# The first conditioning unit and the first chunk of the input projection cover one k-tile in place of two

## The chip, the cores and the metric

The kernel runs on one core of a Trainium2 chip. The metric is the time of one execution in microseconds (us) on the device; the profile of one execution shows what each engine did in it. Engines are called as the profile calls them: PE (matmul), PEld (its weight loads), DVE (VectorE), ACT (ScalarE), POOL (GpSimd), SP (which issues most transfers).

## The reference, cut to what matters

One decoder layer for 256 prompt rows and 8 x 4 sample rows, 288 rows in all, with D = 2048, which is 16 k-tiles of 128. Only its head is touched here.

```
mod = silu(c) @ w_ada + b_ada                 # 2048 x 12288, 9 different c
shift1, scale1, gate1, shift2, scale2, gate2 = split(mod, 6)
h = x * (1 + scale1) + shift1
proj = h @ w_in                               # 2048 x 5120: 40 output tiles of 128
... attention, gated mixing, w_out, norm, ConvFFN, norm
```

k-tile k of h needs columns k of shift1 and scale1, and each of those needs all 2048 rows of w_ada. The layer then goes on to attention, spatial gating, the output projection and a ConvFFN with the much larger w_up and w_down.

## The kernel before, in words

Everything is held transposed: a k-tile of h is 128 partitions by 288 rows. The work is spread over engines by hand; each engine has a list of its own, in order, and semaphores tie the lists.

**Weights in slabs.** w_in, w_out, w_up and w_down come in slabs of 512 KB (128 x 1024 floats, eight 128 x 128 blocks) into `raw`, four slots. ACT rounds a slab to `wH` (`hi`, L1034), DVE takes the rest, `wL = raw - wH` (`lo`, L1441, which counts `split_done`). h is split the same way into `hH` and `hL`. A block then takes three products on PE: hL x wH, hH x wL, hH x wH (L455 to L457, in `products`). A slab is so 24 products.

**The input projection** goes over five chunks of k-tiles, `CHUNKS`: 2, 2, 4, 4, 4. A slab is two k-tiles by four output tiles, ten slabs for each two k-tiles, 80 in all. An output tile of a chunk builds up in one of five PSUM banks (`ps`, banks 0 to 4 in rotation). PE's `take` waits until the bank was released. The first chunk is copied out to `proj` by ACT (L1252), later chunks are added to it by DVE (L1626). For each slab i DVE's list has the adds of slab i and then lo of slab i + 3; ACT's has hi of slab i + 3 and then the copies of slab i, but for slabs 4, 5 and 6, whose hi stands in one go behind the copies of slab 2.

**Conditioning.** w_ada comes in slabs of 512 KB too, through eight slots. A unit (`MOD_UNITS`) gives a few tiles of shift and of scale. Unit 0 is 8 slabs and gives k-tiles 0 and 1; unit 1 is 8 slabs and gives 2 and 3; the others are 16 slabs for four tiles of each. PE does a slab in 16 records of a matmul with 32 columns of weights (L484 for half units, L471 for whole ones). When a unit is complete, ACT copies it to `adaS` (L1046), PE turns it (L512), DVE adds the bias into `modT` (`mod_finish`, L1452) and makes h (`modulate`, L1473 to L1477, into `H32`), ACT makes hH, DVE makes hL. All of unit 0 stands ahead of the first product of the projection. PE fills its waits there with products whose result is not used (`keep_busy`, L584). Later slabs come in bursts of four between two slabs of the projection (`BURSTS`, the slab index behind which each burst stands: 3, 6, 8, 11, ...), and `TURN_AT` is the slab behind which a unit is turned.

**Loads.** SP issues in this order at the start: conditioning 0 to 3, w_in 0, conditioning 4 to 7, x of two k-tiles, w_in 1 to 3. Then for each slab i the conditioning slabs that fit in the ring, and w_in i + 5 when slab i + 1 has been split. One bias product with its own small loads (L610, `bias`) stands behind slab 2.

## Time and profile before

| | us |
|---|---|
| median of 3 runs | 1392.53 (1391.79 to 1394.35) |
| the profiled execution | 1392.78 |
| its span, first to last instruction | 1391.1 |
| PE busy | 1370.0 (98%) |
| DVE busy | 836.8 (60%) |
| ACT busy | 570.4 (41%) |

The profile's busy time of PE is modelled at the end of each matmul, so the starts of matmuls are the better measure of pace. A timeline merges instructions of a kind that follow each other; the bracket behind a row is the time that the engine sat idle before it and what ended the wait. DMA engines are shared by all queues. 0.2% of the median is 2.8 us.

### The profile page before, as it was taken

How to read it: one execution, taken by the hardware profiler on the slowest of the kernel's cores; microseconds unless marked ns; L12 is line 12 of the kernel's file. 1: busy time of each engine (PE TensorE's matmuls, PEld its weight loads, DVE VectorE, ACT ScalarE, POOL GpSimd, SP SyncE). 2: the span in 40 equal slices, each digit the busy share in tenths (PEclk: the TensorE clock that was granted, in tenths of full speed). 3: DMA queues.
4: the chain of work that ended last, by engine and by line, in shares of the span. 5: the costliest groups of instructions: out<-in, count | busy, mean ns of one | idle time of the engine just before them, and what ended most of it. 6: DMA issues, size and time to landing. Idle time of an engine off the chain costs nothing.

```text
span 1391.1 us, 29223 instructions
## 1 busy us (share of the span) xinstructions
PE 1370.0 (98%) x11397; PEld 1297.9 (93%) x11397; DVE 836.8 (60%) x1404; ACT 570.4 (41%) x848; POOL 105.9 (8%) x250
## 2 busy tenths in 40 slices
PE   7999999999999999999999999999999999999996
PEld 5999898899889888999999999999999999999996
DVE  2475556568876569555665544665665544766755
ACT  4533223254643236633444333443444333444433
POOL 1000000004221000000110000110110000101000
PEclk9999999999999999999999999999999999999998
DMA  9999988975888988885545455455455555455541
GB/s 371 409 339 392 343 332 321 342 276 184 300 310 324 366 310 327 290 306 177 166 141 181 162 166 167 151 162 169 151 169 171 160 164 166 149 178 163 169 150 68
DMA packets 89907, 324.94 MB, mean 234 GB/s; under 512 B 10653, under 2 KB 10653, under 8 KB 89440
## 3 DMA queue, kind: packets, MB, share of 16 engines
q1 hardware_dynamic: 82512, 297.34, 60.4%
q0 software_dynamic: 6880, 24.10, 5.1%
q10 hardware_dynamic: 432, 2.33, 0.4%
q8 instruction: 60, 0.98, 0.3%
q14 instruction: 23, 0.19, 0.0%
HBM read 318.05 MB, written 5.67 MB: 233 GB/s over the span
## 4 chain that ended last, share of the span: by engine, by line
PE 94%; DVE 3%; ACT 1%; issue 1%; DMA 1%; SPq 0%; DVEq 0%; ACTq 0%
PE ps L455 28%; PE ps L456 28%; PE ps L457 28%; PE ps L471 5%; PE ps L798 1%; DVE xT L1886 1%; DVE wL L1441 1%; PE ps L484 1%; PE ps L712 1%; DMA ada<-w_ada 1%; PE ps L662 0%; PE ps L584 0%; DVE xT L1897 0%; ACT wH L1034 0%; PE ps L545 0%
## 5 line engine op out<-in xcount | busy, mean ns | idle before, releaser
L1441 DVE TENSOR_TENSOR wL<-raw,wH 128x1024 fp32r<-128x1024 f32 x372 | 449.6, 1218 | 362.7 <-ACT wH L1034 360.6
L1034 ACT ACTIVATE wH<-raw 128x1024 fp32r<-128x1024 f32 x372 | 389.5, 1053 | 593.5 <-PE ps L457 558.7
L455 PE MATMUL ps<-hL,wH 128*128 128x288 f32 x2016 | 602.6, 299 | 0.9 <-DVE hL L1610 0.5
L456 PE MATMUL ps<-hH,wL 128*128 128x288 f32 x2016 | 600.3, 298 | 0.0
L457 PE MATMUL ps<-hH,wH 128*128 128x288 f32 x2016 | 599.7, 297 | 0.0
L455 PEld LDWEIGHTS ps<-hL,wH 128*128 128x128 f32 x2016 | 380.7, 189 | 15.0 <-issue 10.9
L456 PEld LDWEIGHTS ps<-hH,wL 128*128 128x128 f32 x2016 | 379.9, 188 | 0.5 <-issue 0.5
L457 PEld LDWEIGHTS ps<-hH,wH 128*128 128x128 f32 x2016 | 379.1, 188 | 0.0
L455 PE MATMUL ps<-ffL,wH 128*128 128x288 f32 x688 | 204.8, 298 | 0.0
L456 PE MATMUL ps<-ffH,wL 128*128 128x288 f32 x688 | 203.3, 295 | 0.0
L457 PE MATMUL ps<-ffH,wH 128*128 128x288 f32 x688 | 202.7, 295 | 0.0
L1626 DVE TENSOR_TENSOR proj<-ps,proj 128x288 f32<-128x288 f32 x160 | 71.2, 456 | 106.2 <-PE ps L457 105.7
L455 PEld LDWEIGHTS ps<-ffL,wH 128*128 128x128 f32 x688 | 129.0, 188 | 1.0 <-DVE xT L2012 1.0
L457 PEld LDWEIGHTS ps<-ffH,wH 128*128 128x128 f32 x688 | 129.7, 189 | 0.0
L456 PEld LDWEIGHTS ps<-ffH,wL 128*128 128x128 f32 x688 | 129.2, 188 | 0.0
L455 PE MATMUL ps<-mix,wH 128*128 128x288 f32 x256 | 78.3, 306 | 0.4 <-DVE xT L1712 0.2
L456 PE MATMUL ps<-mix,wL 128*128 128x288 f32 x256 | 75.6, 295 | 0.0
L457 PE MATMUL ps<-mix,wH 128*128 128x288 f32 x256 | 75.5, 295 | 0.0
L2191 POOL COPY E<-U 128x4 f32 (+1 forms) x44 | 9.9, 225 | 734.6 <-ACT U L1347 734.6
L455 PEld LDWEIGHTS ps<-mix,wH 128*128 128x128 f32 x256 | 48.1, 188 | 6.3 <-issue 5.4
L457 PEld LDWEIGHTS ps<-mix,wH 128*128 128x128 f32 x256 | 48.2, 188 | 0.0
L456 PEld LDWEIGHTS ps<-mix,wL 128*128 128x128 f32 x256 | 48.1, 188 | 0.0
(261 smaller groups left out, 972.4 us busy)
## 6 DMA issues: line engine op xcount, KB each, us to landing
raw<-w_up SPq DMA_DIRECT2D x168, 512.0 KB, 3.5
ada<-w_ada SPq DMA_DIRECT2D x96, 512.0 KB, 6.4
raw<-w_down SPq DMA_DIRECT2D x83, 512.0 KB, 3.5
raw<-w_in SPq DMA_DIRECT2D x80, 512.0 KB, 7.3
adaX<-w_ada SPq DMA_DIRECT2D x40, 512.0 KB, 5.4
adaY<-w_ada SPq DMA_DIRECT2D x40, 512.0 KB, 7.2
raw<-w_out SPq DMA_DIRECT2D x32, 512.0 KB, 5.7
KV<-keys POOLq DMA_DIRECT2D x16, 512.0 KB, 5.6
```

The costliest lines, as they stand in the source:

```text
L455: nc.tensor.matmul(out, wH[:, w:w + P], rhs_lo(kk), start=start, stop=False)
L456: nc.tensor.matmul(out, wL[:, w:w + P], rhs_hi(kk), start=False, stop=False)
L457: mm = nc.tensor.matmul(out, wH[:, w:w + P], rhs_hi(kk), start=False, stop=stop)
L471: mm = nc.tensor.matmul(ps[32 * c:32 * c + 32, bank, 0:256], cT[:, 32 * k:32 * k + 32], src[:, 256 * c:256 * (c + 1)], start=(k == 0), sto ...
L484: mm = nc.tensor.matmul(ps[32 * c:32 * c + 32, bank, 0:P], cT[:, 32 * k:32 * k + 32], src[:, 512 * kk + P * c:512 * kk + P * (c + 1)], sta ...
L712: mm = nc.tensor.matmul(ps[32 * hq:32 * hq + 32, hh, 0:P], PTm[:, o:o + 32], KV[buf][:, kt * 1024 + h * P:kt * 1024 + (h + 1) * P], start= ...
L798: mm = nc.tensor.transpose(b[0:n, t * P:(t + 1) * P], tile(S4, t, r * P, r * P + n), ident)
L1034: nc.scalar.activation(wH[:, o:o + cols], raw[:, o:o + cols], ACT.Copy).then_inc(hi_done, 1)
L1441: vec_tt(wL[:, o:o + cols], raw[:, o:o + cols], wH[:, o:o + cols].bitcast(F32), ALU.subtract).then_inc(split_done, 1)
L1626: release(vec_tt(tile(proj, n), ps[:, k % 5, 0:ROWS], tile(proj, n), ALU.add), ("in", c, k))
L1886: steps.link(vec_tt(x, x, spread(b[:, 0:1], [0, 2], [1, ROWS]), ALU.mult))
L2191: copy(spread(e, [18, halves], [1, 2]), spread(U[:, o + SEQ:o + SEQ + 1], [UW, halves], [1, 2]))
```

## The change

Unit 0 is split into two units of four slabs: unit 0 gives k-tile 0, the new unit 1 gives k-tile 1, as a burst behind slab 1. The units behind them move up by one number, the bursts that stood behind slab 3 stand behind slab 4. The first chunk is k-tile 0 alone for output tiles 0 to 23, in three slabs of eight tiles by one k-tile. A mixed chunk follows in slabs 3 to 9: four slabs (3, 5, 7, 9) of four new tiles by both k-tiles, copied out by ACT, and between them three (4, 6, 8) of eight tiles by k-tile 1, added by DVE. The number of slabs stays 80. In slabs 0 to 2, DVE copies out tiles 0 to 2 and ACT tiles 3 to 7. Slab 0 is split in two halves. Up to slab 9, DVE's list has lo of slab i + 2 (not i + 3) behind its adds of slab i, and ACT's has hi of slab i + 2 behind its copies of slab i; slabs 12 and 13 are split at slab 10. SP loads conditioning 0 to 3, w_in 0, one tile of x, w_in 1, conditioning 4 and 5, w_in 2, conditioning 6 and 7, x, w_in 3, x. x beyond the fourth k-tile is issued at slab 9 in place of 7, the bias product stands behind slab 11, and POOL's later loads wait for k-tiles 2 and 3 of h. The weights are laid out in memory in the new order.

```
-CHUNKS = [(0, 2), (2, 2), (4, 4), (8, 4), (12, 4)]
+CHUNKS = [(0, 1), (0, 2), (2, 2), (4, 4), (8, 4), (12, 4)]
 LAST = len(CHUNKS) - 1
+ALONE = 24
 LAST_ORDER = [8, 9, 6, 7, 4, 5, 0, 1, 2, 3]
-def group_of(c, p):
-    return LAST_ORDER[p] if c == LAST else p
-IN_SLABS = [(c, g, half) for c, (_, nk) in enumerate(CHUNKS) for g in range(IN_GROUPS) for half in range(nk // 2)]
+def in_slabs():
+    out = [(0, 0, 1, p, 8, True, True) for p in range(0, ALONE, 8)]
+    p = 0
+    for n in (4, 8, 4, 8, 4, 8, 4):
+        out.append((1, 0, 2, p, n, True, True) if n == 4 else (1, 1, 1, p, n, True, True))
+        p += n
+    for c, (k, nk) in enumerate(CHUNKS[2:], 2):
+        for g in range(IN_GROUPS):
+            for half in range(nk // 2):
+                out.append((c, k + 2 * half, 2, 4 * g, 4, half == 0, half == nk // 2 - 1))
+    return out
+IN_SLABS = in_slabs()
 IN_N = len(IN_SLABS)
+MIXED = [t for j in range(3) for t in [*range(ALONE + 4 * j, ALONE + 4 * j + 4), *range(8 * j, 8 * j + 8)]] + [*range(ALONE + 12, ALONE + 16)]
+def in_tile(c, p):
+    if c == 1:
+        return MIXED[p]
+    return 4 * LAST_ORDER[p // 4] + p % 4 if c == LAST else p
+def in_bank(c, p):
+    return (p + 1) % 5 if c == 0 else p % 5
+IN_TD = [sum(n - 1 for _, _, _, _, n, _, stop in IN_SLABS[:s] if stop) for s in range(IN_N + 1)]
...
+HALF, QUARTER = 8, 4
 ADA_RING, BURST = 8, 4
-MOD_UNITS = [(0, HALF, 0, 16), (8, HALF, 2, 18), (16, 16, 4, 20), (32, 16, 8, 24), (48, 16, G1, G1 + 4), (64, 16, 12, 28),
-             (80, 16, G1 + 8, G1 + 12), (96, 16, SH2, SH2 + 4), (112, 16, SC2, SC2 + 4), (128, 16, SH2 + 8, SH2 + 12),
+MOD_UNITS = [(0, QUARTER, 0, 16), (4, QUARTER, 1, 17), (8, HALF, 2, 18), (16, 16, 4, 20), (32, 16, 8, 24), (48, 16, G1, G1 + 4),
+             (64, 16, 12, 28), (80, 16, G1 + 8, G1 + 12), (96, 16, SH2, SH2 + 4), (112, 16, SC2, SC2 + 4), (128, 16, SH2 + 8, SH2 + 12),
              (144, 16, SC2 + 8, SC2 + 12)]
-GATE_UNITS = (4, 6)
-U_LAST_IN, U_SC2, U_SH2B, U_SC2B = 7, 8, 9, 10
-Q_UP = 11
-PARTS = {1: (1,), 2: (2, 3), 3: (4, 5), 5: (6, 7)}
-BURSTS = [3, 6, 8, 11, 14, 16] + [19 + 5 * k // 2 for k in range(20)] + [S_OUT + 15] + [S_OUT + 17 + 2 * k for k in range(7)]
+GATE_UNITS = (5, 7)
+U_SC2, U_SH2B, U_SC2B = 9, 10, 11
+Q_UP = 12
+PARTS = {2: (1,), 3: (2, 3), 4: (4, 5), 6: (6, 7)}
+BURSTS = [1, 4, 6, 8, 11, 14, 16] + [19 + 5 * k // 2 for k in range(20)] + [S_OUT + 15] + [S_OUT + 17 + 2 * k for k in range(7)]
...
+            def ada_quarter_slab(slot, turn, j, copies, bank):
+                if j == 0 and copies:
+                    pe.wait_ge(adaS_ready, copies)
+                pe.wait_ge(ada_in[slot], turn * 16 + 16)
+                src = ada_slot(slot)
+                for kk in range(2):
+                    for c in range(4):
+                        k = 4 * j + 2 * kk + c // 2
+                        mm = nc.tensor.matmul(ps[32 * c:32 * c + 32, bank, 0:P], cT[:, 32 * k:32 * k + 32], src[:, 512 * kk + P * c:512 * kk + P * (c + 1)],
+                                              start=(j == 0 and kk == 0), stop=(j == QUARTER - 1 and kk == 1))
+                mm.then_inc(ada_used, 1)
...
-            for a in range(HALF):
+            for a in range(QUARTER):
                 ada_next(a)
-                if a >= 2:
+                if a >= 1:
                     keep_busy(ps[:, 0, :], 1)
             pe.wait_ge(small_in, 16 * 2)
             ada_turn(0, ("turn", 0), blocks=1)
-            keep_busy(ps[:, 0, :], 4)
-            for i, (c, g, half) in enumerate(IN_SLABS):
-                k0, nk = CHUNKS[c]
-                k = k0 + 2 * half
-                arriving = None
+            keep_busy(ps[:, 0, :], 3)
+            def second_half(t, kk):
+                if t == 4:
+                    pe.wait_ge(split_done, 1)
+            def second_turn(t, kk):
+                if t == 2:
+                    ada_turn(1, ("turn", 1), blocks=1)
+            for i, (c, k, nk, p0, n, start, stop) in enumerate(IN_SLABS):
                 if i == 0:
-                    arriving = lambda kk: pe.wait_ge(h_ready if kk else h_first, 1)
-                elif g == 0:
+                    pe.wait_ge(h_first, 1)
+                elif i == ALONE // 8:
+                    pe.wait_ge(h_ready, 1)
+                elif c > 1 and p0 == 0:
                     pe.wait_ge(h_ready, k // 2 + 1)
-                banks = [(4 * g + t) % 5 for t in range(4)]
-                products(i, i, lambda kk: tile(hH, (k + kk) % H_SLOTS), lambda kk: tile(hL, (k + kk) % H_SLOTS), banks, half == 0, half == nk // 2 - 1,
-                         taking=lambda t: take(pe, ("in", c, 4 * g + t), banks[t]), arriving=arriving, by_k=i == 0)
+                banks = [in_bank(c, p0 + t) for t in range(n)]
+                products(i, i, lambda kk: tile(hH, (k + kk) % H_SLOTS), lambda kk: tile(hL, (k + kk) % H_SLOTS), banks, start, stop, ktiles=nk,
+                         taking=lambda t: take(pe, ("in", c, p0 + t), banks[t]), between={0: second_half, 2: second_turn}.get(i))
...
-            for a in range(HALF):
-                if a == HALF // 2:
-                    load(0, io["w_in"], 0, 0)
+            def load_x(k, n):
+                sp.dma_start(xT[:, k * ROWS:(k + n) * ROWS], io["xT"][:, k * ROWS:(k + n) * ROWS]).then_inc(x_in[k], 16)
+            for a in range(QUARTER):
                 load_ada(a, a)
-            sp.dma_start(xT[:, 0:2 * ROWS], io["xT"][:, 0:2 * ROWS]).then_inc(x_in, 16)
-            for s in range(1, RING):
-                load(s, io["w_in"], s, s)
-            issued = HALF
+            load(0, io["w_in"], 0, 0)
+            load_x(0, 1)
+            load(1, io["w_in"], 1, 1)
+            for a in range(QUARTER, QUARTER + 2):
+                load_ada(a, a)
+            load(2, io["w_in"], 2, 2)
+            for a in range(QUARTER + 2, 2 * QUARTER):
+                load_ada(a, a)
+            load_x(1, 1)
+            load(3, io["w_in"], 3, 3)
+            load_x(2, 2)
+            issued = 2 * QUARTER
             for i in range(-1, S_UP[0]):
-                limit = ada_through(i - 2) + (BURST if i < 2 else ADA_RING)
+                limit = ada_through(i - 2) + ADA_RING if i > 1 else issued + 2 * (i >= 0)
...
-            hi(0, 0, 0)
             unit_copy(0)
+            act.wait_ge(raw_in[0], 16)
+            nc.scalar.activation(wH[:, 0:SLAB // 2], raw[:, 0:SLAB // 2], ACT.Copy).then_inc(hi_first, 1)
             act.wait_ge(h32_first, 1)
             nc.scalar.activation(tile(hH, 0), tile(H32, 0), ACT.Copy).then_inc(hH_first, 1)
+            nc.scalar.activation(wH[:, SLAB // 2:SLAB], raw[:, SLAB // 2:SLAB], ACT.Copy).then_inc(hi_done, 1)
+            def in_copy(i, t):
+                c, p0 = IN_SLABS[i][0], IN_SLABS[i][3]
+                in_filled(act, i, t)
+                release(nc.scalar.activation(tile(proj, in_tile(c, p0 + t)), ps[:, in_bank(c, p0 + t), 0:ROWS], ACT.Copy), ("in", c, p0 + t))
+            def in_hi(s):
+                hi(s, s // RING, s % RING)
+            in_hi(1)
+            for t in range(3, 8):
+                in_copy(0, t)
+            in_hi(2)
+            for t in range(3, 8):
+                in_copy(1, t)
+            unit_copy(1)
+            in_hi(3)
+            in_copy(2, 3)
             act.wait_ge(h32_ready, 1)
             nc.scalar.activation(tile(hH, 1), tile(H32, 1), ACT.Copy).then_inc(hH_ready, 1)
-            hi(1, 0, 1)
-            act.dma_start(xT[:, 2 * ROWS:4 * ROWS], io["xT"][:, 2 * ROWS:4 * ROWS]).then_inc(x_in, 16)
-            hi(2, 0, 2)
-            for i in range(IN_N + 1):
-                if i not in (1, 2, IN_N):
-                    hi_ahead(0, 0, i)
+            for t in range(4, 8):
+                in_copy(2, t)
+            in_hi(4)
+            for i in range(3, IN_N + 1):
+                if 10 < i < IN_N:
+                    in_hi(i + AHEAD)
                 if i in TURN_AT:
                     unit_copy(TURN_AT[i])
-                if i < IN_GROUPS:
-                    for t in range(4):
-                        k = 4 * i + t
-                        if t < 3:
-                            act.wait_ge(tile_done, 3 * i + t + 1)
-                        else:
-                            act.wait_ge(used, i + 1)
-                        release(nc.scalar.activation(tile(proj, k), ps[:, k % 5, 0:ROWS], ACT.Copy), ("in", 0, k))
-                if i == 2:
-                    hi_ahead(0, 0, 1)
-                    hi_ahead(0, 0, 2)
-                if i == 7:
+                if i < 10:
+                    if IN_SLABS[i][2] == 2:
+                        for t in range(4):
+                            in_copy(i, t)
+                    in_hi(i + 2)
+                if i == 10:
+                    in_hi(12)
+                    in_hi(13)
...
+            def modulate_one(k, signal):
+                dve.wait_ge(x_in[k], 16)
+                dd = by_seq(tiles(H32, k, 1, SEQ, ROWS), 1)
+                a, b = (16 + k) * MODS, k * MODS
+                steps.link(vec_tt(dd, by_seq(tiles(xT, k, 1, SEQ, ROWS), 1), mods(16 + k, 1)[1], ALU.mult))
+                vec_tt(dd, dd, mods(k, 1)[1], ALU.add)
+                vec_ts(tile(H32, k, 0, SEQ), tile(xT, k, 0, SEQ), modT[:, a:a + 1], modT[:, b:b + 1], ALU.mult, ALU.add).then_inc(signal, 1)
+            def mod_finish_one(k):
+                b = filled(dve, ("turn", k))
+                out = spread(modT[:, k * MODS:k * MODS + 1], [16 * MODS, 2], [1, MODS])
+                steps.link(vec_tt(out, spread(b[:, 0:1], [32, 2], [1, MODS]), spread(vec[:, V_ADA + k:V_ADA + k + 1], [16, 2], [0, MODS]), ALU.add))
+                release(vec_tt(out, out, spread(b[:, 64:65], [32, 2], [1, MODS]), ALU.add), ("turn", k))
+                released(dve, ("turn", k))
...
-            lo(0, 0)
-            mod_finish(("turn", 0), (0, 16), n=2)
-            dve.wait_ge(x_in, 16)
-            modulate(0)
+            mod_finish_one(0)
+            modulate_one(0, h32_first)
+            dve.wait_ge(hi_first, 1)
+            vec_tt(wL[:, 0:SLAB // 2], raw[:, 0:SLAB // 2], wH[:, 0:SLAB // 2].bitcast(F32), ALU.subtract).then_inc(lo_first, 1)
             dve.wait_ge(hH_first, 1)
             vec_tt(tile(hL, 0), tile(H32, 0), tile(hH, 0).bitcast(F32), ALU.subtract).then_inc(h_first, 1)
+            dve.wait_ge(hi_done, 1)
+            vec_tt(wL[:, SLAB // 2:SLAB], raw[:, SLAB // 2:SLAB], wH[:, SLAB // 2:SLAB].bitcast(F32), ALU.subtract).then_inc(split_done, 1)
+            for i in range(2):
+                for t in range(3):
+                    in_copy(i, t)
+                lo(i + 1, i + 1)
+            in_copy(2, 0)
+            in_copy(2, 1)
+            mod_finish_one(1)
+            modulate_one(1, h32_ready)
+            in_copy(2, 2)
+            lo(3, 3)
             dve.wait_ge(hH_ready, 1)
             vec_tt(tile(hL, 1), tile(H32, 1), tile(hH, 1).bitcast(F32), ALU.subtract).then_inc(h_ready, 1)
-            lo(1, 1)
-            lo(2, 2)
-            for i in range(IN_N + 1):
+            lo(4, 4 % RING)
+            for i in range(3, IN_N + 1):
                 if i < IN_N:
-                    c, g, half = IN_SLABS[i]
-                    if c and half == CHUNKS[c][1] // 2 - 1:
-                        for t in range(4):
-                            k = 4 * g + t
-                            if t < 3:
-                                dve.wait_ge(tile_done, 3 * (IN_GROUPS * c + g) + t + 1)
-                            else:
-                                dve.wait_ge(used, i + 1)
-                            n = 4 * group_of(c, g) + t
-                            release(vec_tt(tile(proj, n), ps[:, k % 5, 0:ROWS], tile(proj, n), ALU.add), ("in", c, k))
-                if i < IN_N - 1:
+                    c, _, nk, _, n, _, stop = IN_SLABS[i]
+                    if stop and (c > 1 or nk == 1):
+                        for t in range(n):
+                            in_add(i, t)
+                if i < 10:
+                    lo(i + 2, (i + 2) % RING)
+                if i == 10:
+                    lo(12, 12 % RING)
+                    lo(13, 13 % RING)
+                if 10 < i < IN_N - 1:
                     lo(i + AHEAD, (i + AHEAD) % RING)
...
-            pool.wait_ge(h32_ready, 1)
+            pool.wait_ge(h32_ready, 2)
```

## Rows read from the trace of the kernel before

**Rows 1.** The page, part 1: busy time, share of the span, instructions.
```profile
PE 1370.0 (98%) x11397; PEld 1297.9 (93%) x11397; DVE 836.8 (60%) x1404; ACT 570.4 (41%) x848; POOL 105.9 (8%) x250
```

**Rows 2.** Table of windows: length, busy of each engine, PEclk, DMA share, GB/s.
```profile
25.00:60.00 35.00, 35.00 (x371) 32.21 (x370) 13.88 (x18) 22.26 (x46) 0.59 (x1) 1.00 1.03 409
```

**Rows 3.** Timeline of PE from 0 to 20.7: start us, length us, what.
```profile
6.46 1.93 PE L484 MATMUL ps<-ada,cT 128*32 128x128 f32 x32 [6.46 <-ACT cT L1230]
9.24 1.08 PE L484 MATMUL ps<-ada,cT 128*32 128x128 f32 x16 [0.84 <-DMA ada<-w_ada]
10.25 1.22 PE L584 MATMUL ps<-cT 128*128 128x256 f32 x2
11.40 1.08 PE L484 MATMUL ps<-ada,cT 128*32 128x128 f32 x16
...
13.42 0.64 PE L484 MATMUL ps<-adaX,cT 128*32 128x128 f32 x16
```

**Rows 4.** Tile cT from 12.4 to 13.4: ns shortest/median/longest, first and last start.
```profile
L584 PE MATMUL ps<-cT x2: 487/640/793, 12.4 to 13.0; 128*128 128x256 f32 x2
```

**Rows 5.** Timeline of SP's queue from 0 to 110: when transfers were issued.
```profile
3.63 0.50 SPq L944 DMA_DIRECT2D raw<-w_in  x1
...
6.96 1.64 SPq L944 DMA_DIRECT2D raw<-w_in  x3
```

**Rows 6.** DMA issues at 3.63 and at 6.96: KB, us from issue to landing.
```profile
raw<-w_in SPq DMA_DIRECT2D x1, 512.0 KB, 8.1
...
raw<-w_in SPq DMA_DIRECT2D x1, 512.0 KB, 12.0
```

**Rows 7.** Timeline of all engines from 17 to 21.
```profile
17.03 0.64 PE L484 MATMUL ps<-adaY,cT 128*32 128x128 f32 x16
...
17.74 0.28 ACT L1046 ACTIVATE adaS<-ps 128x128 f32<-128x128 f32 x1 [4.91 <-PE ps L484]
...
18.50 0.26 DVE L1452 TENSOR_TENSOR modT<-ps,vec 128x18 f32<-128x18 f32 x2 [4.33 <-PE ps L512]
...
19.20 0.73 DVE L1477 TENSOR_SCALAR H<-xT,modT 128x256 f32<-128x256 f32 x2
19.64 0.44 ACT L1234 ACTIVATE hH<-H 128x288 fp32r<-128x288 f32 x1 [1.62 <-DVE H L1477]
...
20.11 0.46 DVE L1610 TENSOR_TENSOR hL<-H,hH 128x288 fp32r<-128x288 f32 x1 [0.19 <-ACT hH L1234]
...
20.72 0.38 PE L455 MATMUL ps<-hL,wH 128*128 128x288 f32 x1 [0.53 <-DVE hL L1610]
```

**Rows 8.** Timeline of PE around a burst, and around the turn of unit 1.
```profile
34.41 0.30 PE L457 MATMUL ps<-hH,wH 128*128 128x288 f32 x1
...
36.52 0.41 PE L455 MATMUL ps<-hL,wH 128*128 128x288 f32 x1
36.76 0.29 PE L456 MATMUL ps<-hH,wL 128*128 128x288 f32 x1
...
51.70 0.27 PE L512 MATMUL ps<-cst,adaS 128*128 128x128 f32 x1
```

**Rows 9.** Timelines of PE, ACT and DVE where slab 2 ends.
```profile
30.25 0.29 PE L457 MATMUL ps<-hH,wH 128*128 128x288 f32 x1
...
30.58 0.41 ACT L1252 ACTIVATE proj<-ps 128x288 f32<-128x288 f32 x1 [0.38 <-PE ps L457]
30.89 3.06 ACT L1034 ACTIVATE wH<-raw 128x1024 fp32r<-128x1024 f32 x3
...
31.97 3.50 DVE L1441 TENSOR_TENSOR wL<-raw,wH 128x1024 fp32r<-128x1024 f32 x3 [7.08 <-ACT wH L1034]
```

**Rows 10.** Timeline of DVE from 6 to 110.
```profile
64.09 1.22 DVE L1441 TENSOR_TENSOR wL<-raw,wH 128x1024 fp32r<-128x1024 f32 x1
65.22 1.37 DVE L1626 TENSOR_TENSOR proj<-ps,proj 128x288 f32<-128x288 f32 x3
...
95.24 1.55 DVE L1626 TENSOR_TENSOR proj<-ps,proj 128x288 f32<-128x288 f32 x4
```

More of the change, by code:

```diff
@@ L424, in width, with in_filled @@
             return ROWS if k < 8 else SEQ
+        def in_filled(eng, s, t):
+            if t < IN_SLABS[s][4] - 1:
+                eng.wait_ge(tile_done, IN_TD[s] + t + 1)
+            else:
+                eng.wait_ge(used, s + 1)
         def in_done(eng, p):
@@ L440, in products @@
             def products(s, i, rhs_hi, rhs_lo, banks, first, last, ktiles=2, taking=None, arriving=None, by_k=False, between=None):
-                pe.wait_ge(split_done, s + 1)
+                if isinstance(s, int) and s == 0:
+                    pe.wait_ge(lo_first, 1)
+                else:
+                    pe.wait_ge(split_done, s + 1)
                 n = len(banks)
@@ L491, in ada_next @@
                 first, n, _, _ = MOD_UNITS[q]
-                step = ada_half_slab if n == HALF else ada_slab
-                if a == MOD_UNITS[2][0]:
-                    released(pe, "bias")
+                step = {QUARTER: ada_quarter_slab, HALF: ada_half_slab}.get(n, ada_slab)
                 if a == MOD_UNITS[U_SC2][0]:
@@ L1050, in unit_copy @@
                 a, n, _, _ = MOD_UNITS[q]
-                ada_copy(a + n, ada_bank(q), ("turn", q - 1) if q else None, cols=P if n == HALF else 256)
+                ada_copy(a + n, ada_bank(q), ("turn", q - 1) if q else None, cols=256 if n == 16 else P)
             def h_hi(p):
@@ L1642, in _ @@
                         modulate(PARTS[q][0])
[L1643 removed]
+                if i == 13:
                     b = filled(dve, "bias")
@@ L2225, in rows_t @@
         return f(x.T.reshape(-1, P, ROWS).transpose(1, 0, 2).reshape(P, -1))
-    w_in = a["w_in"][0].reshape(KT, P, IN_GROUPS, 4, P)
-    w_in_s = f(np.stack([w_in[CHUNKS[c][0] + 2 * half:CHUNKS[c][0] + 2 * half + 2, :, group_of(c, g)].transpose(1, 0, 2, 3).reshape(P, -1)
-                         for c, g, half in IN_SLABS]))
+    w_in = a["w_in"][0].reshape(KT, P, 4 * IN_GROUPS, P)
+    w_in_s = f(np.stack([w_in[k:k + nk][:, :, [in_tile(c, p0 + t) for t in range(n)]].transpose(1, 0, 2, 3).reshape(P, -1)
+                         for c, k, nk, p0, n, _, _ in IN_SLABS]))
     w_out = a["w_out"][0]
@@ L2256, in ada_slab_of @@
         _, n, first, second = unit
+        if n == QUARTER:
+            return np.concatenate([w_ada[tile_of(4 * j + 2 * kk + odd), cols(t, 1)] for kk in range(2) for odd in range(2) for t in (first, second)], 1)
         if n == HALF:
```

33 lines of the change are left out of this document (20 added, 13 removed).

## The prediction

> **What bounds the kernel now.** I read the page's first part before anything else: PE is busy for nearly the whole span [rows 1]. In the table of windows the stretch right behind the start shows PE without a gap while the DMA engines are full [rows 2]. So what counts is when the first product starts, how much work PE does after it, and where PE has to wait. The timeline of PE gives the first: PE starts at 6.46, works through eight conditioning slabs, each as it lands, and begins the first product of the projection at 20.72 [rows 3, 7]. From there to the end of the third slab at 30.38 (30.25 and one spacing of 0.13) it needs 9.66 us, 3.22 us a slab and 0.40 us for the three products that one k-tile gives to one output tile [rows 7, 9]. The chain of work follows PE almost all the way to the end, so I take a delay near the start to reach the end whole.
>
> **Part 1, the earlier start.** Unit 0 needs four conditioning slabs in place of eight. The third landed at 9.24, when PE took it up [rows 3]. The first slab of w_in was issued at 3.63 and took 8.1 us: 11.7 [rows 5, 6]. The fourth conditioning slab lies between, at about 10.5. SP issues these five in the same order as now. The second w_in slab landed at 6.96 + 12.0 = 19.0, behind four conditioning slabs and 288 KB of x; that makes 1.3 us for each 512 KB [rows 5, 6]. In the new order this gives landings of about 12.1 for the tile of x, 13.4 (w_in 1), 14.7 and 16.0 (conditioning 4, 5), 17.3 (w_in 2), 18.6 and 19.9 (6, 7), 20.3 (x), 21.6 (w_in 3).
>
> PE reaches conditioning slab 3 later than it lands, because slabs 0 and 1 end at 8.4 and a keep-busy product now follows slab 1 as well. One conditioning slab takes 1.01 us and a keep-busy product 1.15 us early on; after 13.4 a slab takes 0.57 us [rows 3]. The granted clock reads 1.00, that is 2.4 GHz, but those durations are nearly two to one, like 1.2 to 2.4 GHz, and one keep-busy product shows the step inside it: its first half took 793 ns and its second, at 13.0, 487 [rows 4]. Before that step PE had worked without a gap since 9.24. Now it works without one from 6.46. If the step comes as long after the gapless work began (3.8 us), it is at 10.2, slab 3 runs from 11.1 to 11.7; if it stays at 13.0, slab 3 ends at 12.7 (8.4 + 1.15 + 1.01 + 1.15 + 1.01). From the end of the last slab (17.60) to the first product (20.72) the kernel now takes 3.12 us: ACT's copy at 17.74, VectorE's at 18.50, ScalarE's hH at 19.64, hL at 20.11 [rows 7]. The new path has the same links; the half lo beside hH adds some 0.1 us. So the first product starts at 14.9 or at 16.0 (the late keep-busy product adds 0.1). I take the middle, 15.4: **-5.3 us**, ends -5.8 and -4.7.
>
> **Part 2, what moves behind the start.** Unit 1's four slabs now run as a burst behind slab 1. A burst moves the next slab from 34.54 to 36.52, and the product behind it starts 0.24 us later in place of 0.13: **+2.1 us** [rows 8]. They land by 19.9 and are wanted from about 21.9, so they cost no wait. One more transposition of 0.27 us, most of it hidden under the neighbours [rows 8]: **+0.1**. The product for the bias moves from slab 2 to slab 11 and costs the same there. The number of products and of slabs is unchanged.
>
> **Part 3, the first wait, for k-tile 1.** Call B the start of slab 2. VectorE copies tiles 0 and 1 of it (until B + 1.56, with 0.46 for a copy, by its add from PSUM [rows 10]), makes the factors and h of k-tile 1 (1.14 us, from 18.50 to 19.64 [rows 7]), copies tile 2 (to B + 3.0), does lo of slab 3 (next instruction 1.13 us later [rows 10], B + 4.1), hL (0.46), and 0.15 us later PE can start: B + 4.6. Without it slab 3 would start at B + 3.4. **+1.3 us** with the slow first product. Ends: 1.0 if VectorE's copies take only the 0.36 us at which its adds follow each other [rows 10], 1.6 if each of the three handovers between engines takes 0.1 us longer. The trace of before has no copy of such a tile on VectorE; the add is the nearest row.
>
> **Part 4, the waits for banks in the mixed chunk.** This is the part that decides. Slabs 4, 6 and 8 hold eight tiles by one k-tile. PE opens a new bank every 0.40 us and there are five, so tile 5 needs VectorE's add of tile 0 at S + 2.0, S being the start of the slab. But VectorE's list has lo of slab i + 2 before the adds of slab i + 1, and in the slabs before these (3, 5, 7) ScalarE does its split only behind its four copies. That chain is in the trace: PE ended a slab at 30.38, ScalarE copied the last tile at 30.58, started the split at 30.89, VectorE started lo at 31.97 [rows 9], which is S + 1.59. The instruction behind a lo starts 1.13 us later, an add takes 0.46 and PE needs 0.15 more: S + 3.33. So PE stands for 1.3 us, and its first product is 0.1 slower: 1.4 us in slab 4 and in slab 6, **+2.8**. Behind that the adds come every 0.36 us (1.55 for four [rows 10]), faster than PE's tiles, so it is one wait a slab.
> At slab 8 unit 2's factors and k-tiles 2 and 3 of h stand between lo and the adds. They take from 18.50 to 19.93 [rows 7], 1.34 us with the overlap. The turn before it gives back 0.1: **+2.6**. Queued behind the waiting VectorE are only its adds and lo of slab 10, whose user is two slabs away. Where the blocked order costs nothing is from slab 10 on: all tiles have two k-tiles, PE opens a bank every 0.8 us, and tile 5 comes at S + 4.0. SP's loads from slab 7 on wait for later splits than now, but by the same cadence each lands 5 us or more before its use: slabs 7 to 9 by about 40, wanted from 45 on.
> Bounds for each wait: below, 0.9 us if the handovers between engines are free; above, 1.9 if ScalarE takes the 0.5 us between the end of a slab and its split a second time.
>
> **The sum:** -5.3 + 2.1 + 0.1 + 1.3 + 2.8 + 2.6 = +3.6 us. The profiled run took 1392.78 us (span 1391.1); the median is 1392.53. 1392.5 + 3.6 = **1396.1 us**, 0.26% slower. 0.2% (2.8 us) is about what a measurement can tell from no change.
>
> **Rivals.**
> *The waits for banks do not come* (the other sign). That needs VectorE's first add of slabs 4, 6 and 8 to end before S + 2.0, 1.2 us earlier than worked out, for instance because the splits ran ahead. Then -5.3 + 2.1 + 0.1 + 1.3 = -1.8 us, 1390.7; with no wait for k-tile 1 and the early clock step -3.6, 1388.9. For it: today PE never waits here [rows 2]. Against it: order and bank count are fixed in the code, and today each tile has 0.8 us. It decides as soon as the three waits sum to less than 1.8 us.
> *Data late.* If transfers land 2 us later than at 1.3 us each, slabs 1 and 2 or unit 1's burst wait as well: +1.5 to +3, 1397.6 to 1399. For it: the DMA engines are full throughout [rows 2]. Against it: 2 us of slack at every point.
> *The start comes less early*, at about 17, since ScalarE and VectorE now do half splits between the links: 1397.7.
> *The clock falls in the new gaps.* Work at the slower level took 1.01 us against 0.57 [rows 3]; for one slab of 3.2 us that is +2.5 us, 1398.6 with one fall. Against it: the granted clock stays 1.00 in [rows 2], and before the step a gap of 0.8 us at 8.4 was followed by slow work that had been slow already, so it shows nothing.
> The Trainium skill ("TensorE: Matmul & The Clock Gate", section "A second HAM failure mode: psum-queue depth-cycling") says that a PE which pauses briefly between groups while it cycles through PSUM banks can fall back to half rate again and again. By it this kernel would lie at that rival's time or above. No gap of this kind is in the trace of before, so it neither agrees nor disagrees.
>
> **How the numbers follow.** Waits as worked out: 0.68, at 1396.1, own range 1394.6 to 1397.7 (0.5 us for the clock step either way, about 1 us for the waits together). No waits for banks: 0.12. Data late: 0.08. Less early: 0.06. Clock: 0.06. To leave out less than 2 in 10 the range goes from 1391.5 to 1399.0. Slower by over 0.2% means above 1395.3: 0.46 of the first case's 0.68, and the last three: 0.66. Faster by over 0.2% needs the far end of the second: 0.05. The same: 0.29.
>
> **What the next profile would show.** First projection product (PE on hL) at 14.9 to 16.0. A gap of PE of about 1.2 us ahead of slab 3, ended by VectorE's hL. In slabs 4 and 6 a gap of about 1.3 us behind the fifth tile, ended by a VectorE add from PSUM, and one of about 2.5 us in slab 8. VectorE's lo of slabs 5, 7 and 9 released by ScalarE's split, that by PE. From slab 10 on no gap that was not there before. I am wrong if PE shows no such gaps, or if DMA ends them.

## The result and the profile after

The changed kernel takes 1396.07 us (median of 9 executions, 1393.1 to 1398.77) against 1392.53 before (9, 1391.54 to 1394.35): ratio 1.0025, 95% interval 1.0014 to 1.0035. It is slower by 3.5 us. The profiled execution is one of the slowest, 1398.77 us with a span of 1397.1.

PE has the same work as before ([rows 1]):

```profile
PE 1370.6 (98%) x11390; PEld 1298.3 (93%) x11390; DVE 848.6 (61%) x1442; ACT 568.5 (41%) x841; POOL 107.4 (8%) x250
```

The timeline of PE at the start, which answers to [rows 3] and [rows 7] (start us, length us, what, and in brackets the idle time and what ended it):

```profile
6.50 1.93 PE L534 MATMUL ps<-ada,cT 128*32 128x128 f32 x32 [6.50 <-ACT cT L1294]
8.36 1.22 PE L632 MATMUL ps<-cT 128*128 128x256 f32 x2
9.51 1.08 PE L534 MATMUL ps<-ada,cT 128*32 128x128 f32 x16
10.52 1.22 PE L632 MATMUL ps<-cT 128*128 128x256 f32 x2
11.68 1.08 PE L534 MATMUL ps<-ada,cT 128*32 128x128 f32 x16
12.68 0.72 PE L632 MATMUL ps<-cT 128*128 128x256 f32 x2
...
15.84 0.40 PE L492 MATMUL ps<-hL,wH 128*128 128x288 f32 x1 [1.00 <-DVE hL L1720]
...
22.21 0.29 PE L494 MATMUL ps<-hH,wH 128*128 128x288 f32 x1
...
24.32 0.40 PE L492 MATMUL ps<-hL,wH 128*128 128x288 f32 x1
...
28.86 0.40 PE L492 MATMUL ps<-hL,wH 128*128 128x288 f32 x1 [0.84 <-DVE hL L1734]
```

The first product starts 4.88 us earlier than at 20.72. Conditioning slab 3 begins at 11.68, later than it can have landed, and PE steps to its full pace only behind it. Slab 1 of the projection ends at 22.34 (22.21 and one spacing of 0.13), slab 2 begins at 24.32, and slab 3 waits for hL of k-tile 1 until 28.86.

The view of the waits, PE from 0 to 400 (in all, times, longest):

```profile
PE ps L492 <- DVE proj L1590: 4.5, 3, 2.3
PE ps L492 <- DVE hL L1720: 1.0, 1, 1.0
PE ps L492 <- DVE hL L1734: 0.8, 1, 0.8
```

Three waits for a DVE add from PSUM, 4.5 us. How the first comes about is in the timelines of three engines, which answer to [rows 9] and [rows 10]. ACT's:

```profile
32.37 0.41 ACT L1306 ACTIVATE proj<-ps 128x288 f32<-128x288 f32 x1 [0.40 <-PE ps L494]
32.67 2.00 ACT L1098 ACTIVATE wH<-raw 128x1024 fp32r<-128x1024 f32 x2
```

DVE's:

```profile
33.75 1.23 DVE L1523 TENSOR_TENSOR wL<-raw,wH 128x1024 fp32r<-128x1024 f32 x1 [2.93 <-ACT wH L1098]
34.90 3.00 DVE L1590 TENSOR_TENSOR proj<-ps,proj 128x288 f32<-128x288 f32 x8
```

PE's:

```profile
32.17 0.30 PE L492 MATMUL ps<-hL,wH 128*128 128x288 f32 x1
...
34.03 0.29 PE L494 MATMUL ps<-hH,wH 128*128 128x288 f32 x1
35.40 0.40 PE L492 MATMUL ps<-hL,wH 128*128 128x288 f32 x1 [1.08 <-DVE proj L1590]
```

ACT copies the last tile of slab 3, then splits; DVE has been idle for 2.93 us for that split, does lo, and only then the adds; PE, which began slab 4 at 32.17 and ended its fifth tile at 34.16 (34.03 and one spacing), opens the sixth at 35.40. In slab 8 the factors of k-tiles 2 and 3 lie between, on DVE:

```profile
53.41 1.23 DVE L1523 TENSOR_TENSOR wL<-raw,wH 128x1024 fp32r<-128x1024 f32 x1 [4.55 <-ACT wH L1098]
54.56 0.25 DVE L1534 TENSOR_TENSOR modT<-ps,vec 128x18 f32<-128x18 f32 x2
...
55.89 3.00 DVE L1590 TENSOR_TENSOR proj<-ps,proj 128x288 f32<-128x288 f32 x8
```

and PE opens its tile behind the first of these adds:

```profile
56.40 0.40 PE L492 MATMUL ps<-hL,wH 128*128 128x288 f32 x1 [2.31 <-DVE proj L1590]
```

Behind this gap the table of windows (length, busy of PE, PEld, DVE, ACT, POOL, PEclk, DMA share, GB/s) shows what [rows 2] did not:

```profile
56.00:57.00 1.00, 0.60 (x4) 0.61 (x5) 1.00 (x4) 0.69 (x1) 0.74 (x2) 1.00 1.00 401
57.00:58.00 1.00, 1.00 (x7) 0.99 (x5) 1.00 (x4) 0.00 (x0) 1.00 (x3) 0.57 1.04 421
58.00:59.00 1.00, 1.00 (x10) 0.40 (x12) 1.00 (x4) 0.00 (x0) 0.94 (x2) 0.50 0.33 110
59.00:60.00 1.00, 1.00 (x16) 0.42 (x11) 1.00 (x2) 0.00 (x0) 0.00 (x0) 0.50 0.85 220
60.00:61.00 1.00, 1.00 (x20) 0.49 (x12) 0.69 (x2) 0.00 (x0) 0.00 (x0) 0.73 0.71 282
```

The granted clock goes to 0.50, 1.2 GHz, at about 57.1 and stays there for some 3.4 us. The burst behind slab 8 takes 3.03 us; the one of [rows 8] took 1.98:

```profile
58.27 3.03 PE L508 MATMUL ps<-ada,cT 128*32 128x256 f32 x32
```

Where the two profiles stand at one point far behind the change, the product for the gate rows in slab 49 (before, then after):

```profile
222.33 1.12 PE L520 MATMUL ps<-wsT,ones 128*128 128x512 f32 x2
```

```profile
227.51 1.12 PE L568 MATMUL ps<-wsT,ones 128*128 128x512 f32 x2
```

5.18 us apart. From there to the end of the span they differ by 0.8 us more (1391.1 - 222.33 = 1168.8, 1397.1 - 227.51 = 1169.6).

### The profile page after: what moved, and what is told of

The parts are those of the page before. It is cut to its first block, busy times and chain, and to the rows that moved or that the text cites. A ratio compares the mean times of both kernels' runs of the same rounds, so it can differ in the third digit from the quotient of the medians.

```text
span 1397.1 us, 29221 instructions
## 1 busy us (share of the span) xinstructions
PE 1370.6 (98%) x11390; PEld 1298.3 (93%) x11390; DVE 848.6 (61%) x1442; ACT 568.5 (41%) x841; POOL 107.4 (8%) x250
## 4 chain that ended last, share of the span: by engine, by line
PE 93%; DVE 4%; ACT 1%; issue 1%; DMA 0%; DVEq 0%; ACTq 0%
PE ps L492 28%; PE ps L493 27%; PE ps L494 27%; PE ps L508 5%; DVE wL L1523 1%; PE ps L853 1%; DVE xT L2006 1%; PE ps L767 1%; ACT wH L1098 1%; PE ps L534 0%; PE ps L717 0%; DMA cT<-cT 0%; DVE xT L2017 0%; PE ps L521 0%; PE ps L593 0%
## 5 line engine op out<-in xcount | busy, mean ns | idle before, releaser
L1590 DVE TENSOR_TENSOR proj<-ps,proj 128x288 f32<-128x288 f32 x184 | 79.5, 453 | 102.5 <-PE ps L494 102.1
```

The costliest lines, as they stand in the source:

```text
L1590: release(vec_tt(out, ps[:, in_bank(c, p0 + t), 0:ROWS], out, ALU.add), ("in", c, p0 + t))
```

## The experiments

Each was compared with runs of the kernel before on the same chip, so the difference to those is what is compared from one row to another. It is +3.5 for the changed kernel. The interval of each ratio is some 2.5 us wide, so two differences less than about 2 us apart are not told from each other by their medians alone.

| run | median us (executions) | kernel before beside it | difference | ratio, 95% |
|---|---|---|---|---|
| hi first | 1390.38 (11) | 1392.73 | -2.4 | 0.9976 to 0.9994 |
| hi first, slab 3 early | 1390.34 (11) | 1392.73 | -2.4 | 0.9971 to 0.9989 |
| fill behind the wait | 1399.75 (5) | 1392.73 | +7.0 | 1.0038 to 1.0065 |
| late factors | 1394.46 (11) | 1392.73 | +1.7 | 1.0008 to 1.0026 |
| fill all gaps | 1396.02 (11) | 1392.56 | +3.5 | 1.0016 to 1.0034 |
| fill the long gap | 1395.68 (11) | 1392.56 | +3.1 | 1.0012 to 1.0029 |
| early products | 1397.91 (6) | 1392.56 | +5.4 | 1.0019 to 1.0044 |
| hi first, slab 3 early, early products | 1389.37 (11) | 1392.56 | -3.2 | 0.9970 to 0.9987 |
| only the long gap | 1391.71 (12) | 1391.6 | +0.1 | 0.9995 to 1.0012 |
| late factors, x at slab 7 | 1393.32 (11) | 1391.6 | +1.7 | 1.0001 to 1.0018 |
| the changed kernel again | 1395.15 (10) | 1391.6 | +3.6 | 1.0013 to 1.0032 |
| before, early products | 1392.33 (11) | 1391.6 | +0.7 | 0.9995 to 1.0013 |

**Hi first.** The order that made the waits, turned round on ACT:

```
                 if i < 10:
+                    in_hi(i + 2)
                     if IN_SLABS[i][2] == 2:
                         for t in range(4):
                             in_copy(i, t)
-                    in_hi(i + 2)
```

> The changed kernel with one order turned round: in slabs 3, 5, 7 and 9 ScalarE splits slab i + 2 before its four copies, not behind them. Theory of the order: VectorE is no longer blocked, the gaps of PE in slabs 4 and 6 (1.1 us each) go and that of slab 8 (2.3 us) falls under 0.5 us, since only the factors of k-tiles 2 and 3 still stand ahead of the adds. With them goes the fall of the clock behind slab 8. Against the changed kernel about -4.7 us and up to -6; against the kernel before 1390.5 to 1391.5. The gap of 0.8 us ahead of slab 3 stays. Rival (the order is not it, five banks are too few for one tile each 0.40 us, or transfers are late): the gaps stay and the time stays at 1394 to 1397.

The median is 5.9 us less than the changed kernel's by the differences, where 4.7 and up to 6 were forecast. In the view of the waits (0 to 300) no wait for an add is left, also not in slab 8:

```profile
PE ps L492 <- DVE hL L1720: 1.0, 1, 1.0
PE ps L492 <- DVE hL L1734: 0.8, 1, 0.8
PE ps L576 <- ACT proj L1126: 0.8, 1, 0.8
```

The rival is out: with this order five banks are enough, and up to 300 us no wait of PE is ended by a transfer. The order made all three waits. The gate rows stand at 219.35, 3.0 us earlier than in the kernel before; this profile's first product began at 14.49.

**Hi first, slab 3 early.** The same edit, and slab 3's split earlier on both engines:

```
+            in_hi(3)
             unit_copy(1)
-            in_hi(3)
             in_copy(2, 3)
...
+            lo(3, 3)
             in_copy(2, 0)
...
             in_copy(2, 2)
-            lo(3, 3)
             dve.wait_ge(hH_ready, 1)
```

> As the run before (ScalarE's split ahead of its copies), and slab 3 is split before unit 1 is copied and turned: hi ahead of ScalarE's copy of unit 1, lo ahead of VectorE's first copy of slab 2, in the 2.9 us in which VectorE had nothing to do. Theory: the chain to h of k-tile 1 loses one lo (1.13 us), so the wait ahead of slab 3 (0.84 us idle, some 1.1 with the slow start) nearly goes: another -1.0 us, 1389.5 to 1390.5 in all. Rival (the wait is set by hH and hL of k-tile 1 whatever stands beside them, or w_in 3 lands too late for the earlier split): the gap stays at 0.8, no gain over the run before.

The wait for hL of k-tile 1 is gone:

```profile
PE ps L492 <- DVE hL L1720: 1.0, 1, 1.0
PE ps L576 <- ACT proj L1126: 0.7, 1, 0.7
```

The median does not show it (1390.34 to 1390.38). In the profiles the gate rows are at 219.27 with the first product at 15.03, against 219.35 with 14.49: counted from the first product that is 0.62 us less, where 1.0 was expected. It is below what these medians can tell.

**Fill behind the wait.** A first try at closing the gaps with work, products called ahead of tile 5 of slabs 4, 6 and 8:

```
+            def fill_gap(n):
+                return lambda t, kk: keep_busy(ps[:, 5, :], n) if t == 5 else None
...
-between={0: second_half, 2: second_turn}.get(i)
+between={0: second_half, 2: second_turn, 4: fill_gap(2), 6: fill_gap(2), 8: fill_gap(5)}.get(i)
```

> The changed kernel with its gaps filled: before tile 5 of slabs 4, 6 and 8 PE does 2, 2 and 5 products whose result is not used (0.47 us each). No wait is taken away. Theory of the clock: in the profile of the changed kernel the granted clock fell to 0.50 from 57.2 to 60.5, right behind the gap of slab 8, and cost 1.5 us; with the gap filled it stays at 1.00. The median falls by the share of executions in which it falls, 0.5 to 1.5 us, and the spread (1393.1 to 1398.8 for the changed kernel) shrinks towards that of the kernel before (1391.5 to 1394.4). Rival (the fall is a matter of the whole load or of chance, not of the gap): median and spread stay, and the clock may still be seen to fall.

The place was wrong. The call comes behind the wait for the bank, so the gaps stayed at 4.5 us and nine products of 0.47 us, 4.2 us, were added to them: +3.5 measured. The granted clock fell here too (0.55 in the window from 58 to 60).

**Late factors.** `mod_finish` and `modulate` of k-tiles 2 and 3 behind DVE's adds of slab 8:

```
                         for t in range(n):
                             in_add(i, t)
+                if i == 8:
+                    mod_finish(("turn", 2), (2, 18), n=2)
+                    modulate(1)
...
-                if i in TURN_AT:
+                if i in TURN_AT and i != 7:
```

> The changed kernel with one move: VectorE makes the factors and h of k-tiles 2 and 3 behind its adds of slab 8, not ahead of them. Theory: the gap of slab 8 falls from 2.3 to 1.1 us like those of slabs 4 and 6, -1.2 us; if the fall of the clock comes from the long gap, it goes as well, for -1.2 to -2.7 us against the changed kernel: 1393.3 to 1394.8. Rival (the clock falls by the sum of the gaps, not by the longest): -1.2 us alone, and a fall of the clock can still be seen. Rival (unit 2's work is off the path): no change.

The gap of slab 8 is 0.97 us, the granted clock stays at 1.00 behind it and the median falls by 1.8. But the profile has a new wait, here in PE's timeline:

```profile
78.79 0.40 PE L492 MATMUL ps<-hL,wH 128*128 128x288 f32 x1 [1.58 <-DVE proj L1590]
```

and what is ahead of it, in ACT's:

```profile
76.05 1.06 ACT L1098 ACTIVATE wH<-raw 128x1024 fp32r<-128x1024 f32 x1 [10.90 <-DMA raw<-w_in]
```

w_in landed at 76.0, ACT split it, DVE's lo stood ahead of its adds and PE waited for the add: the same chain with DMA at its head.

**Fill all gaps, fill the long gap.** The filling products ahead of tile 4, so that they run while DVE is late: in slabs 4, 6 and 8, or in slab 8 alone (there the table has only `8: fill_gap(5)`). Against the try before:

```
-                return lambda t, kk: keep_busy(ps[:, 5, :], n) if t == 5 else None
+                return lambda t, kk: keep_busy(ps[:, 5, :], n) if t == 4 else None
```

> The changed kernel with products whose result is not used ahead of tile 4 (not of tile 5 as in the first try, where they came behind the wait and cost their full 4.2 us): 2, 2 and 5 of them in slabs 4, 6 and 8, 0.47 us each. They lie in the gaps and take none away. Theory of the clock: granted clock 1.00 all through 40 to 66, the burst behind slab 8 takes 1.9 us and not 3.0, the median falls from 1396.1 to about 1395, the slowest runs (1398.8) go. If all time that the clock takes is a matter of that one fall, the spread is that of the kernel before, 3 us. Rival (the fall has another cause): it is seen again, median and spread as for the changed kernel, or up by the 0.1 to 0.3 us by which the products outlast the gap.

> As the run before with only the long gap filled, in slab 8; the two of 1.1 us in slabs 4 and 6 stay open. Theory (only the long gap lets the clock fall): the same as with all filled, about 1395, no fall in the profile. Rival (any of the gaps can, the long one only did so in the one profile there is): falls behind slab 4 or 6 in some executions, median 0.3 to 0.8 us above the run with all filled.

In both profiles the granted clock stays at 1.00 up to 1380 us, and the gate rows are at 225.72 and 225.63 with first products at 15.80 and 15.50: 1.7 and 1.5 us less than after, counted from the first product (227.51 - 15.84 = 211.67, 209.92 and 210.13). So in a profile the fall costs about the 1.5 us read from it. The medians, +3.5 and +3.1, are hardly below +3.5, and the forecast of 1395 was too low. The executions span 2.9 and 3.5 us, against 5.7 for the changed kernel here but only 3.6 when it was run again below, so a narrower spread is not shown either. How often the clock falls in the other executions can be read another way, from the mean granted clock of each (see "What it missed").

**Early products.** Eight products on a constant tile while PE waits for c, in the changed kernel, in the one with hi first and slab 3 early, and in the kernel before:

```
-            nc.vector.memset(ones[:, :], 1.0)
+            nc.vector.memset(ones[:, :], 1.0).then_inc(ones_set, 1)
...
+            pe.wait_ge(ones_set, 1)
+            for k in range(8):
+                nc.tensor.matmul(ps[:, 0, 0:P], ones[:, :], ones[:, :], start=True, stop=True)
             pe.wait_ge(c_silu, 1)
```

> The changed kernel with 8 products on a constant tile from 1.7 us on, while PE waits for c; nothing else differs. Theory (the place at which PE steps to its full clock sets the first product): starts of the first projection product have been 15.84, 14.49, 15.03, 14.80 and 14.79 in the five profiles with the same head. With PE at full pace from the first conditioning slab on, slab 3 is bound by its landing at about 10.5 and ends at 11.1, the first product comes at 14.2 to 14.5, -0.6 us against the mean of those, 1395.4. Rival (landing and the chain behind it set it): 14.8 to 15.0 as now, no change. Against both: the warm products outlast the wait for c and push slab 0 back.

> The version that the runs so far point to: ScalarE's splits ahead of its copies, slab 3 split ahead of unit 1's copy, and the early products for the clock. Theory: 1390.3 less 0.6 us, 1389.7, with the first product at 14.2 to 14.5 and no gap of PE from there to 270. Rival (transfers are the next bound: in the run with the late factors PE stood for 1.6 us at 78.8 behind a w_in slab that landed late): a gap of PE appears between 30 and 100, its start ended by a split that waited for DMA, and the time stays at 1390 or above.

> The kernel before with the 8 early products on a constant tile. Theory: its first product waits for conditioning slab 7, which lands at 17.0, and the clock has stepped up by 13.4 anyway, so nothing changes: first product at 20.7, 1392.5. That the step lies on the path is new in the changed kernel, where PE is late for slab 3. Rival (the step is worth as much here): first product 0.5 us or more earlier.

The timelines of PE, first with early products alone, then with all three edits:

```profile
1.75 3.79 PE L637 MATMUL ps<-ones 128*128 128x128 f32 x16 [1.75 <-DVE ones L1710]
6.43 1.94 PE L535 MATMUL ps<-ada,cT 128*32 128x128 f32 x32 [0.90 <-ACT cT L1298]
...
10.46 0.81 PE L633 MATMUL ps<-cT 128*128 128x256 f32 x2
```

```profile
1.75 3.44 PE L637 MATMUL ps<-ones 128*128 128x128 f32 x16 [1.75 <-DVE ones L1710]
6.45 1.39 PE L535 MATMUL ps<-ada,cT 128*32 128x128 f32 x32 [1.26 <-ACT cT L1298]
...
14.10 0.40 PE L493 MATMUL ps<-hL,wH 128*128 128x288 f32 x1 [1.01 <-DVE hL L1724]
```

The same products did not raise PE's pace in the first case (1.94 us for two conditioning slabs, the step at about 10.9, first product 14.94) and did so in the second (1.39, first product 14.10, the earliest seen). The first kernel is at +5.4 with five of six executions at 1397.5 to 1398.0 and one at 1393.4, where a gain of 0.6 was forecast; its profile has the fall of the clock. Its interval (1.0019 to 1.0044) overlaps those of the changed kernel (1.0014 to 1.0035 and 1.0013 to 1.0032), so that it is slower than without the products, or has the fall more often, is not shown. The last kernel is the fastest, -3.2, where 1389.7 was expected and 1389.37 came; against hi first and slab 3 early (-2.4) the 0.8 us are too little for these medians. In the kernel before, the early products change nothing that can be measured; its first product came at 21.03.

The forecast for the last kernel had no gap of PE from the first product to 270, and there is one. Slab 3 of w_in is there for ACT only at 21.94; its lo now stands ahead of DVE's copies, and PE waits in slab 2 for a bank that such a copy frees:

```profile
21.94 1.06 ACT L1102 ACTIVATE wH<-raw 128x1024 fp32r<-128x1024 f32 x1 [0.74 <-DMA raw<-w_in]
```

```profile
26.47 0.40 PE L493 MATMUL ps<-hL,wH 128*128 128x288 f32 x1 [0.72 <-DVE proj L1587]
```

So the rival of this run, that transfers are the next bound, holds in part. Far behind, two conditioning slabs come late, and the granted clock falls again, here without any long gap:

```profile
515.19 0.64 PE L509 MATMUL ps<-ada,cT 128*32 128x256 f32 x8 [1.00 <-DMA ada<-w_ada]
516.44 0.89 PE L509 MATMUL ps<-ada,cT 128*32 128x256 f32 x8 [0.61 <-DMA ada<-w_ada]
```

```profile
516.00:518.00 2.00, 1.56 (x11) 0.90 (x12) 1.93 (x5) 0.47 (x2) 0.00 (x0) 0.67 1.03 406
518.00:520.00 2.00, 2.00 (x10) 2.00 (x10) 1.93 (x5) 1.80 (x4) 0.00 (x0) 0.50 1.01 414
```

This profiled execution is the slowest of its 11, 1392.71 us.

**Only the long gap.** Hi first in slabs 3 and 5, not in slab 7:

```
                 if i < 10:
+                    if i < 7:
+                        in_hi(i + 2)
                     if IN_SLABS[i][2] == 2:
                         for t in range(4):
                             in_copy(i, t)
-                    in_hi(i + 2)
+                    if i >= 7:
+                        in_hi(i + 2)
```

> The changed kernel with ScalarE's split ahead of its copies in slabs 3 and 5 only; slab 7 stays as it is. Theory: the gaps in slabs 4 and 6 go, -2.4 us against the changed kernel, the gap of 2.3 us in slab 8 stays, and the clock falls behind it as in the three profiles that had this gap so far (1.5 us in that execution). Median 1393.0 to 1394.0. Rival (the fall needs the gaps ahead of it too): the gap is there, the granted clock stays at 1.00 behind it, median about 1392.5 to 1393.

The gap of 2.31 us in slab 8 is there alone, and behind it, in the windows from 54, the clock stays:

```profile
54.00:56.00 2.00, 2.00 (x35) 1.04 (x33) 2.00 (x5) 0.00 (x0) 1.43 (x3) 1.00 0.59 168
56.00:58.00 2.00, 2.00 (x18) 1.86 (x15) 1.17 (x2) 0.41 (x1) 0.00 (x0) 1.00 0.74 221
```

The median of 1391.71 lies below the 1393.0 to 1394.0 of the theory and nearer to its rival. It is 3.5 us below the changed kernel's, where the two gaps of slabs 4 and 6 are worth some 2.5. One profile cannot say whether the fall needs the earlier gaps or just did not happen.

**Late factors, x at slab 7.** As late factors, and ACT issues the load of x two slabs earlier:

```
-                if i == 9:
+                if i == 7:
                     act.dma_start(xT
...
```

> The run with the late factors of k-tiles 2 and 3, and the 1.77 MB of x issued at slab 7 again, not at 9. There PE stood for 1.6 us at 78.8 behind slab 15 of w_in, which landed at 76.0. Theory (the block of x stands ahead of that slab in the DMA engines): with x two slabs (8 us) earlier slab 15 lands up to 4 us earlier, the gap goes, -1.6 us against that run in the profile. Rival (SP issued slab 15 late, since it waits for a split): the gap stays about 1.6 us.

The wait at 78.8 is gone from the profile, as the theory has it, but the difference to the kernel before is the same, +1.7. Counted from the first product, slab 49 comes 2.0 us earlier than with late factors alone (224.42 - 15.85 = 208.57 against 225.41 - 14.81 = 210.60). Either that wait was not in most executions or something of its size took its place; the profile shows no other wait of PE from slab 8 up to 100.

**The changed kernel again.** No edit.

> The changed kernel itself once more, for its spread beside the others and a second profile of it. Median 1395.5 to 1396.5, span of the runs 4 to 6 us. Theory of the clock: the granted clock falls to 0.50 behind the gap of slab 8 in this profile as well, and the first product starts between 14.5 and 15.9. Rival: the fall was a single event, the profile shows none.

The median is 1395.15, a little under the 1395.5 to 1396.5 of the forecast, as is that of the kernel before beside it; the executions span 3.6 us, under the 4 to 6. The profile has the same three waits of 4.5 us in all, the first product at 15.44, and the clock falls again at the gap of slab 8, which ends at 56.02:

```profile
54.00:56.00 2.00, 0.00 (x0) 0.00 (x0) 1.93 (x9) 0.37 (x1) 0.12 (x1) 1.00 0.99 399
56.00:58.00 2.00, 1.99 (x8) 1.99 (x9) 1.92 (x6) 0.32 (x1) 2.00 (x4) 0.51 1.00 400
58.00:60.00 2.00, 2.00 (x23) 1.02 (x25) 1.74 (x3) 0.00 (x0) 0.57 (x2) 0.64 0.73 234
```

## Why the prediction was right

**Part 1, the start, was right.** 14.9 to 16.0 was forecast, with 15.4 taken. The ten profiles whose head is the changed one without early products have 14.49 to 15.85, mean 15.25. The place of the step in PE's pace makes the difference, as argued: with the step behind conditioning slab 3 it is 15.84, with it ahead of slabs 2 and 3, as in the profile of hi first, 14.49:

```profile
9.55 0.65 PE L534 MATMUL ps<-ada,cT 128*32 128x128 f32 x16
...
10.76 0.64 PE L534 MATMUL ps<-ada,cT 128*32 128x128 f32 x16
```

Neither time that the prediction offered for the step, 10.2 or 13.0, is a rule: PE worked without a gap from 6.5 in both profiles, and the step came at about 9.5 in one and 12.7 in the other.

**Part 2.** From the end of slab 1 at 22.34 to the first product of slab 2 at 24.32 the burst took 1.98 us, and 0.1 behind it, as forecast.

**Part 3, the wait for k-tile 1.** B + 4.6 was forecast, 28.86 - 24.32 = 4.54 came; the terms as written add up to 4.7 (3.0 + 1.13 + 0.46 + 0.15). Its chain was confirmed by hi first with slab 3 early, where one lo less in it takes the wait away.

**Part 4, the banks.** DVE's adds start 2.73 us behind the start of slab 4 (34.90 - 32.17) and 1.24 us pass between the fifth and the sixth tile, 1.3 with the slow first product; 1.4 was forecast. In slab 8 the idle gap is 2.31 us, with the two edges 2.6. Hi first removes all three and turns +3.5 into -2.4: it is shown that they are the loss. What each cost can be read at slab 49, counted from the first product: 204.86 without the waits (219.35 - 14.49), 207.43 with the long one alone (222.42 - 14.99), so 2.6 as forecast; 208.57 with three of about 1 us and no fall of the clock, so 1.24 each where 1.4 was forecast. The rival without bank waits gave 1390.7 as its time; that is the time of the kernel in which they were taken away, 1390.38.

**What it missed.** The fall of the clock was a rival with 0.06 and was set apart from the main case. It came together with it: in both profiles of the changed kernel, and in two more with the same gap. What I held against it was a granted clock of 1.00 in a stretch without gaps, which says nothing on gaps. By its terms the sum for the profiled execution is -4.9 + 2.1 + 0.1 + 1.2 + 2.7 + 2.6 = +3.8 at slab 49; +5.2 was measured, and the fall is the other 1.4. The price given for this rival, 2.5 us, was too high as well: against the filled kernels a fall cost 1.7 and 1.5. The Trainium skill ("TensorE: Matmul & The Clock Gate", section "A second HAM failure mode: psum-queue depth-cycling") tells of a bf16 kernel that pauses often between groups of products as it cycles through PSUM banks, and whose rate goes down and up again for it. The traces here agree in part: four show one fall each at the gap of slab 8, none again and again, and those with the long gap alone or with gaps of about 1 us show none there.

How often the clock falls in the other executions is shown in part by the mean granted clock that is recorded for each. At half rate for 3.4 us it drops by 0.0012. It reads 0.995 in 9 of the 19 executions of the changed kernel (3 of 9, then 6 of 10), and in none of the 66 of hi first, hi first with slab 3 early, the two with late factors, fill all gaps and fill the long gap, nor in any of the 90 of the kernel before that ran beside the experiments. In the second set of the changed kernel those six took 1395.14 to 1397.17 and the other four 1393.55 to 1394.72. It is a rough sign, since an execution with a fall can read 0.996, as the first profile does. With only the long gap 1 of 12 reads 0.995, and it is the slowest, 1395.86. The kernels with early products are left out, since the kernel before reads 0.994 or 0.995 with them in 4 of 11 executions that are no slower than the others. So by this sign the fall comes in about half of the executions of the changed kernel or more. As an estimate, half of a fall's 1.6 us is 0.8 us on the median, and that fits the 5.9 us of hi first: 2.5 for the two short waits, 2.6 for the long one, and the rest. The filled kernels should then have come out 0.8 us lower and were 0.1 and 0.4 lower; their intervals neither bear the estimate out nor exclude it.

That the median still met 1396.1 without this term is so in part luck: -5.5 for the mean start, then +2.1, +0.1, +1.2, +5.1 for the waits and +0.8 make +3.8, near the forecast +3.6 and the measured +3.5, since start, bank waits and the wait for k-tile 1 were each a little better than forecast. The rest of the kernel differs too: from the gate rows of slab 49 to the end the fourteen profiles have 1166.7 to 1171.8 us, the most in the one with the fall at 517. Why the clock falls in some executions and not in others stays open.

**The rival of late data** was right in kind for the next version: as soon as DVE's order was relieved in slab 8 alone, a w_in slab landed late at 76.0. In the kernel with all three edits the split of slab 3 waits for its slab until 21.9. In the changed kernel itself no wait of PE up to 500 us is ended by DMA; the first ones behind that, 0.6 and 0.4 us, are those of the kernel before (0.5 and 0.3).

## What to carry to other kernels

When a stage is cut finer to start earlier, each bank of the accumulator is reused sooner: here every 0.40 us in place of 0.80, and work that had stood ahead of an eviction at no cost became a wait of 1.3 us. Write down, for each engine's list, what the instruction that frees a buffer has to wait behind, on that engine and on the engine that feeds it; one swap of two lines was worth 5.9 us here. An early start is only kept as far as the stage behind it is supplied and drained.

## What the runs showed of the hardware that was not expected

Around a PE gap of 2.31 us that followed two of 1.08 us, the granted clock fell to 0.50 for about 3.4 us in four of four profiles, between 0.4 us ahead of the end of the gap (early products) and 1.2 us behind it (fill behind the wait). With the last gap at 0.97 us (two profiles) or filled (two) it stayed at 1.00, and so it did with the first two gaps taken away (one profile). The length of one gap does not decide it: with all three edits two gaps of 1.00 and 0.61 us within 3 us were followed by the same fall. A fall at slab 8 cost about 1.5 to 1.7 us.

At the start the granted clock reads 1.00 while PE works at half pace: 16 records of a conditioning slab took 1.01 us before a step and 0.57 us behind it. With the head of the changed kernel the step came anywhere between 9.5 and 12.7 us in the profiles shown, and the first product between 14.49 and 15.85. Sixteen records on a constant tile from 1.75 us on did not reliably bring it forward: with them it came before 6.5 in one profile, at about 10.9 in another, and in the kernel before behind 14.2, where it had been at 13.0 without them.
